# A transformer layer on one Trainium2 core: expert gate by tanh, normed rows stored modulated, low parts on VectorE, gathered rows handled ahead of the down-projection ring, the reciprocal root on GpSimd

## The chip, the core and the metric

The kernel runs on one core of a Trainium2 chip. The metric is device microseconds of one execution. A profile is one traced execution of the same program; its times are counted from the first instruction of the trace. TensorE has two clock levels, 2.4 and 1.2 GHz; the profile gives the granted level as a share, so 1.00 is 2.4 GHz and 0.50 is 1.2 GHz.

## The reference

One layer of a diffusion transformer over 2048 rows of width 1024 (and 256 context rows), in fp32: a mixer (latent attention with 8 heads, and bidirectional retention with 8 heads), then a mixture of experts in which each of 16 experts picks its own 256 rows, then a final norm.

```python
x = x + ga1 * y                                            # y: mixer output times w_o
h = rmsnorm(x, g_norm_ffn) * (1.0 + sc2) + sh2             # the modulated rows
aff = softmax(h @ w_router)                                # router, 16 experts
g, idx = top_k(swapaxes(aff, 1, 2), cap)                   # 256 rows for each expert
xs = h[idx]
a, u = xs @ w_gate, xs @ w_up                              # 1024 -> 768
y = (silu(a) * u) @ w_down * g                             # 768 -> 1024
x = x + ga2 * scatter_add(idx, y)
out = rmsnorm(x, g_final)
```

## The kernel before

The program is a chain of stages with a barrier between them: `modulation` (the row of `w_ada` products), `project`, `retention`, `attention`, `mix_out`, `experts` (a threshold search, then 16 expert turns) and `final_norm`. Every engine has its own instruction list, written by hand, and engines meet through semaphores; there is no scheduler. Within a list the order is fixed, so one late operation holds back all that stands behind it on its engine.

**Split products.** To keep fp32 accuracy on TensorE, each operand of a large product is split in two: a rounded part (ScalarE copies it to the round format) and a low part (the whole minus the rounded part, a subtraction on VectorE or GpSimd). Each product is three passes. The `whole` copy lies where the low part is written.

**Stage `mix_out`**, 16 tiles of 128 rows. On TensorE a turn m is: the first half of the product of the mixer output and `w_o` (L1280, 24 matmuls), the transposes of the normed rows of tile m-1 (L1289), the second half, the router of tile m-1 (L1297). VectorE adds the residual (L1384, L1386), scales by the reciprocal root (L1392), and after the transposes multiplies and adds the modulation by columns (L1359, L1361). ScalarE takes the sum of squares (L1331) and then the root as Ln and Exp (L1334, L1336). GpSimd makes the low part of the mixer tile (L1269). The unmodulated normed rows go to DRAM as `scratch_xn2`.

**Stage `experts`**, a turn for each expert e. TensorE: six steps `gate_up` of 96 matmuls each (L1614), the slot numbers of expert e+1 after the second (L1590), four blocks of transposes of the rows gathered for e+1 (L1600, two after `gate_up`, one after step 2 of `down` and one after step 3), and twelve steps `down` of six matmuls (L1628). The transposes go to two PSUM banks, 6 and 7, so block n waits until block n-2 has been read. VectorE reads each block with two operations `modulate` (L1818, L1820), ScalarE rounds it (L1665) and VectorE takes the low part (L1826). The gate of step f is exp on ScalarE (L1674) and four operations on VectorE (L1841, L1843 a reciprocal, L1845, L1848), then rounding (L1669) and the low part `rest_hidden` (L1852). Weights: `w_gate` and `w_up` come in three pieces of 2 MB in all each (L1498), the 12 pieces of `w_down` in a ring of six buffers of 256 KB (L1503): piece 6 is asked for when `down` step 0 is finished. Low parts: those of `w_gate` and of the first six pieces of `w_down` on VectorE (`rest_gate` L1830, `rest_down` L1835), those of `w_up` and of the last six pieces on GpSimd (`rest_up` L1540, `rest_down` L1545). GpSimd also issues the gather of e+1 (L1535) and the scatter-add of e (L1559), whose descriptors it writes itself. ScalarE alternates the rounding of `w_down` pieces 6 to 8 with that of gathered blocks 1 to 3.

**Stage `final_norm`**: four groups of four tiles: load, squares on ScalarE (L1966), Ln and Exp (L1969, L1971), scaling on VectorE (L1981), store.

## Time and profile before

| | before |
|---|---|
| median of 3 runs | 3539.53 us (3539.48 to 3540.74) |
| span of the profiled execution | 3526.4 us |
| TensorE matmul busy, share of the span | 3097.0 us, 88% |
| VectorE busy | 2266.7 us, 64% |
| ScalarE busy | 1427.3 us, 40% |
| GpSimd busy | 992.7 us, 28% |
| mean granted TensorE clock | 0.934 |
| HBM traffic over the span | 102 GB/s |

The page of the profile does not give the time of the profiled execution apart from its span. The span is 13.1 us shorter than the median of the runs; it counts from the first to the last instruction. The shares are means over stages with different limits, so the rows shown further down are read for each stage. A row of the window view gives the stretch and its length, then for TensorE, its weight loads, VectorE, ScalarE and GpSimd the busy us (with the number of instructions), the granted clock, the share of DMA time and GB/s. The expert turns begin at 2472.22 us and their last matmul ends at 3461.59 us.

### The profile page before, as it was taken

Reading aid. Unit: us, or ns where it says so; the run is one execution under the profiler, and the core shown is the slowest. Engines: PE = TensorE matmul, PEld = TensorE weight load, DVE = VectorE, ACT = ScalarE, POOL = GpSimd, SP = SyncE. Lnnn points to the kernel's source line nnn. Section 1 sums busy time; section 2 is a strip of 40 time slices with the busy share of each in tenths; the row PEclk is TensorE's granted clock in tenths of the full one; section 3 lists DMA queues with packets and bytes.
Section 4 is the critical chain, followed back from the end, with each engine's and each line's share of the span. In section 5 each row is a group of like instructions: output and inputs, shape, how many; then the busy total and the mean of one; then the engine's idle time right before and its main releaser. Section 6 shows DMA issues by size and latency. Waiting matters only on the chain. (4 is left out here: it accounts for less than half of the span.)

```text
span 3526.4 us, 44830 instructions
## 1 busy us (share of the span) xinstructions
PE 3097.0 (88%) x14689; PEld 2192.4 (62%) x14689; DVE 2266.7 (64%) x2823; ACT 1427.3 (40%) x2136; POOL 992.7 (28%) x514
## 2 busy tenths in 40 slices
PE   6899999999786999999999988971988989899892
PEld 1455555555785556556555647850888878888782
DVE  1133333333675777777777764557888989889893
ACT  0133333332223566666556644330334343333433
POOL 0000001100453332332333212211445444444441
PEclk9999999999776999999999999985999999999996
DMA  8412111121322011011001004341565666656656
GB/s 320 149 59 69 59 59 64 66 67 48 102 89 58 4 31 31 5 31 31 23 13 29 5 20 157 125 141 57 156 203 169 191 186 181 196 165 195 190 145 226
DMA packets 252530, 362.92 MB, mean 103 GB/s; under 512 B 34356, under 2 KB 168503, under 8 KB 250808
## 3 DMA queue, kind: packets, MB, share of 16 engines
q1 hardware_dynamic: 243128, 326.91, 28.5%
q0 software_dynamic: 9216, 33.56, 4.3%
q8 instruction: 113, 1.85, 0.2%
q14 instruction: 73, 0.60, 0.1%
HBM read 278.60 MB, written 81.83 MB: 102 GB/s over the span
## 5 line engine op out<-in xcount | busy, mean ns | idle before, releaser
L465 PE MATMUL bank<-w_in_sb,h_T 128*128 128x512 f32 (+1 forms) x1440 | 610.2, 579 | 2.1 <-DVE h_T L614 2.1
L1614 PE MATMUL ebank<-gathered_T,w_gate_up 128*128 128x256 f32 x4608 | 564.9, 284 | 20.5 <-ACT w_gate_up L1656 12.7
L1614 PEld LDWEIGHTS ebank<-gathered_T,w_gate_up 128*128 128x128 f32 x4608 | 560.2, 190 | 24.4 <-issue 23.5
L1075 PE MATMUL abank<-scores,head_v 128*128 128x512 f32 x1152 | 546.0, 602 | 2.2 <-ACT scores L1113 2.2
L1038 PE MATMUL abank<-head_qT,head_kT 96*128 96x512 f32 x1728 | 504.6, 437 | 22.9 <-POOL head_qT L1017 22.9
L465 PEld LDWEIGHTS bank<-w_in_sb,h_T 128*128 128x128 f32 x1440 | 271.1, 191 | 298.9 <-issue 298.7
L1038 PEld LDWEIGHTS abank<-head_qT,head_kT 96*128 96x128 f32 x1728 | 327.7, 190 | 169.9 <-issue 94.7
L1024 POOL TENSOR_TENSOR scores<-scores,max_for_pool 128x1536 f32<-128x1536 f32 x64 | 221.1, 3476 | 570.9 <-ACT max_for_pool L1107 570.9
L1101 ACT ACTIVATE scores<-abank 128x512 f32<-128x512 f32 x576 | 314.2, 608 | 77.0 <-PE abank L1038 71.2
L1075 PEld LDWEIGHTS abank<-scores,head_v 128*128 128x128 f32 x1152 | 218.6, 194 | 180.3 <-issue 162.8
L1628 PE MATMUL ebank<-w_down,hidden_T 128*128 128x512 f32 x1152 | 303.0, 418 | 21.0 <-POOL w_down L1545 20.8
L1540 POOL TENSOR_TENSOR w_gate_up<-w_gate_up_whole,w_gate_up 128x2048 fp32r<-128x2048 f32 x48 | 229.1, 4773 | 268.2 <-ACT w_gate_up L1656 180.0
L1113 ACT ACTIVATE scores<-scores 128x1536 f32<-128x1536 f32 x192 | 287.3, 1498 | 39.8 <-DVE scores L1155 35.5
L1139 DVE TENSOR_TENSOR score_max<-score_max,scores 128x1536 f32<-128x1536 f32 x128 | 225.1, 1758 | 94.4 <-ACT scores L1101 92.9
L1628 PEld LDWEIGHTS ebank<-w_down,hidden_T 128*128 128x128 f32 x1152 | 223.1, 199 | 80.0 <-POOL w_down L1545 30.2
L1155 DVE TENSOR_TENSOR scores<-scores,abank 128x1536 f32<-128x1536 f32 x128 | 218.1, 1744 | 52.0 <-PE abank L1058 52.0
L582 POOL TENSOR_TENSOR q_rope_terms<-q_rows,rope_rows 128x256 f32<-128x256 f32 x18 | 13.0, 724 | 788.1 <-ACT q_rows L552 788.1
L1674 ACT ACTIVATE gate_exp<-ebank 128x256 f32<-128x256 f32 x96 | 36.9, 384 | 453.2 <-DVE hidden_T L1852 237.9
L1280 PE MATMUL obank<-w_o_sb,mix_tile 128*128 128x512 f32 x768 | 184.7, 397 | 20.5 <-DVE w_o_sb L1399 20.5
L1545 POOL TENSOR_TENSOR w_down<-w_down_whole,w_down 128x512 fp32r<-128x512 f32 x96 | 124.0, 1304 | 275.8 <-ACT w_down L1660 275.2
L1656 ACT ACTIVATE w_gate_up<-w_gate_up_whole 128x2048 fp32r<-128x2048 f32 x96 | 176.3, 1900 | 16.6 <-DMA w_gate_up_whole<-in_w_exp_up 16.6
L1280 PEld LDWEIGHTS obank<-w_o_sb,mix_tile 128*128 128x128 f32 x768 | 143.8, 190 | 50.2 <-issue 21.3
(261 smaller groups left out, 4138.3 us busy)
## 6 DMA issues: line engine op xcount, KB each, us to landing
w_gate_up_whole<-in_w_exp_gate SPq DMA_DIRECT2D x48, 1024.0 KB, 5.9
w_gate_up_whole<-in_w_exp_up SPq DMA_DIRECT2D x48, 1024.0 KB, 9.0
w_down_whole<-in_w_exp_down SPq DMA_DIRECT2D x192, 256.0 KB, 2.9
ada_w<-in_w_ada SPq DMA_DIRECT2D x12, 2048.0 KB, 12.8
scratch_ret<-ret_rows SPq DMA_DIRECT2D x72, 256.0 KB, 2.5
x_tile<-in_x_all SPq DMA_DIRECT2D x18, 512.0 KB
w_in_sb<-in_w_in SPq DMA_DIRECT2D x4, 2048.0 KB, 15.0
chunk_qk<-scratch_ret SPq DMA_DIRECT2D x16, 512.0 KB
```

Of the source, the lines that this page charges most:

```text
L465: m = pe.matmul(banks[bank][:, 0:n], hT[u][:, k, :], w_in[:, k, lo:lo + n], start=(k == 0), stop=(k == KD - 1))
L1024: pool.tensor_tensor(x, x, mid(ms[:, :], G), ALU.subtract).then_inc(sg["shifted_pool"].sem, 1)
L1038: m = pe.matmul(banks[kt % 3][:, :], kT[u][:, kp, k], qT[u][:, qp, q], start=(n == 0), stop=(n == 2))
L1075: m = pe.matmul(banks[5 + j % 2][:, :], v1[u][:, kt, :], sc[j % 2][:, kt, :], start=(kt == 0), stop=(kt == T - 1))
L1101: act.activation(sc[j % 2][:, kt, :], banks[kt % 3][:, :], ACT.Copy).then_inc(sg["scores"].sem, 1)
L1113: act.activation(x, x, ACT.Exp, scale=ATT_SCALE).then_inc(sg["probs"].sem, 1)
L1139: dve.tensor_tensor(mx[:, :, :], mx[:, :, :], s[:, g * G:(g + 1) * G, :], ALU.max).then_inc(sg["max_keys"].sem, 1)
L1155: dve.tensor_tensor(x, x, mid(banks[4][:, :], G), ALU.subtract).then_inc(sg["shifted"].sem, 1)
L1280: x = pe.matmul(banks[2 * u + half][:, :], mt[u][:, mp, k, :], w_o[:, wp, k, half * 512:(half + 1) * 512], start=(k == 0 and n == 0), stop ...
L1540: pool.tensor_tensor(w_gu[c][:, 1, 1], w_gu_whole[c][:, 1, 1], w_gu[c][:, 0, 1].bitcast(F32), ALU.subtract).then_inc(sg["up_rest"].sem, 1)
L1614: x = pe.matmul(banks[f % 3][:, j * CAP:(j + 1) * CAP], w_gu[c][:, wp, j, k, o:o + P], xsT[:, xp, k, :], start=(k == 0 and n == 0), stop=( ...
L1628: x = pe.matmul(banks[Y_BANKS[2 * c + h]][:, :], hid[:, hp, k, h * P:(h + 1) * P], w_d[i % RING][:, wp, :], start=(k == 0 and n == 0), sto ...
```

## The change

Seven edits.

1. **Rows stored modulated.** `modulation` stores the 16 modulation columns (2048 numbers) to DRAM as two rows; the DMA has 128x16 runs of one number. `mix_out` loads them broadcast to all partitions (`ffn_rows`, 1 MB). The normed rows are multiplied and shifted before they are stored and transposed: the one operation L1392 becomes two (L1411, L1414 of the new kernel). The two pairs after the transposes become two copies (L1377), and `modulate` in `experts` goes: ScalarE and VectorE read the gathered block from PSUM.
2. **Mix root on GpSimd.** Ln and Exp on ScalarE become an add and a power of -0.5 on GpSimd (L1283, L1285).
3. **Transposes half a tile later.** TensorE's turn of `mix_out` becomes: first half, router of m-2, second half, transposes of m-1.
4. **Gate by tanh.** silu(a) = 0.5 a (1 + tanh(a/2)): one ScalarE operation and two on VectorE in place of four.
5. **Low parts on VectorE.** All of them: `rest_up` and GpSimd's `rest_down` go to VectorE. GpSimd keeps only gather and scatter in `experts`.
6. **Gathered rows ahead of the down ring.** ScalarE rounds gathered blocks 1 to 3 before pieces 6 to 11 of `w_down`; TensorE transposes the third and fourth block after `down` steps 1 and 2. A transpose block waits for the low part of the block two before.
7. **Final root on GpSimd**, as in 2.

```diff
@@ modulation, SP queue
+            sp.wait_ge(s_fold, 5)
+            sp.dma_start(scratch["ffn_rows"].rearrange("o (j p) -> p (o j)", p=P), perm["modcols"][:, 0, 24:40], allow_slow_non_contiguous=True).then_inc(perm["ffn_rows_stored"], 16)
             sp.wait_ge(s_ga2, 16)
@@ mix_out, GpSimd
+            def turn(m, u, behind, ahead):
+                sg["x2_rstd"].wait(pool, m, 1)
+                sg["x2_normed"].wait(pool, m - 1)
+                settled(pool)
+                pool.tensor_scalar(st[:, 1:2], st[:, 0:1], EPS, None, ALU.add).then_inc(sg["x2_rstd"].sem, 1)
+                sg["x2_rstd"].wait(pool, m, 2)
+                pool.tensor_tensor(st[:, 1:2], st[:, 1:2], power[:, 0:1], ALU.pow).then_inc(sg["x2_rstd"].sem, 1)
+                if ahead:
+                    mix_rest(m + 2, u)
@@ mix_out, TensorE
-                y_half(m, u, 0, first)
-                if not first:
-                    transposes(m - 1)
-                y_half(m, u, 1, first)
-                if not first:
-                    router(m - 1)
+                y_half(m, u, 0, behind == 0)
+                if behind == 2:
+                    router(m - 2)
+                y_half(m, u, 1, behind == 0)
+                if behind:
+                    transposes(m - 1)
@@ mix_out, VectorE
-                dve.tensor_scalar(xn[:, :], x2[u][:, :], st[:, 1:2], None, ALU.mult).then_inc(sg["x2_normed"].sem, 1)
+                dve.scalar_tensor_tensor(xs[:, :], x2[u][:, :], st[:, 1:2], ffn_rows[:, 1, :], ALU.mult, ALU.mult).then_inc(sg["x2_scaled"].sem, 1)
+                sg["x2_scaled"].wait(dve, m)
+                settled(dve)
+                dve.tensor_tensor(xn[:, :], xs[:, :], ffn_rows[:, 0, :], ALU.add).then_inc(sg["x2_normed"].sem, 1)
@@ experts, TensorE
-                sg["modulated"].wait(pe, e, 2 * (n - 2) + 1)
+                sg["gathered_rest"].wait(pe, e, n - 1)
...
-                    if i in (2, 3) and ahead:
-                        transposes(e + 1, i)
+                    if i in (1, 2) and ahead:
+                        transposes(e + 1, i + 1)
@@ experts, ScalarE
-                for i, n in ((6, 1), (7, 2), (8, 3)):
-                    round_down(e, i)
-                    if ahead:
+                if ahead:
+                    for n in range(1, 4):
                         round_gathered(e + 1, n)
-                for i in range(9, ND):
+                for i in range(6, ND):
                     round_down(e, i)
@@ experts, VectorE
-                dve.tensor_scalar(x[:, :], x[:, :], 1.0, None, ALU.add).then_inc(s.sem, 1)
-                s.wait(dve, e, 4 * f + 1)
-                dve.reciprocal(x[:, :], x[:, :]).then_inc(s.sem, 1)
-                s.wait(dve, e, 4 * f + 2)
-                dve.tensor_tensor(x[:, :], banks[f % 3][:, 0:CAP], x[:, :], ALU.mult).then_inc(s.sem, 1)
-                s.wait(dve, e, 4 * f + 3)
+                dve.scalar_tensor_tensor(x[:, :], x[:, :], 1.0, banks[f % 3][:, 0:CAP], ALU.add, ALU.mult).then_inc(s.sem, 1)
+                s.wait(dve, e, 2 * f + 1)
                 sg["d_psum"].wait(dve, e - 1)
-                dve.tensor_tensor(x[:, :], banks[f % 3][:, CAP:], x[:, :], ALU.mult).then_inc(s.sem, 1)
+                dve.scalar_tensor_tensor(x[:, :], x[:, :], 0.5, banks[f % 3][:, CAP:], ALU.mult, ALU.mult).then_inc(s.sem, 1)
```

**VectorE in an expert turn.** The rows of the second half of a turn before, from the low part of hidden step 4 to the fourth gathered block. `hidden_T` rows are `rest_hidden`, `gathered_T` rows the low parts of gathered blocks.

```order
L1852 TENSOR_TENSOR hidden_T<-gate_exp0,hidden_T 128x256
L1818 TENSOR_TENSOR modulated0<-ebank6,mod_cols 128x512
L1820 TENSOR_TENSOR modulated0<-modulated0,mod_cols 128x512
L1852 TENSOR_TENSOR hidden_T<-gate_exp1,hidden_T 128x256
L1818 TENSOR_TENSOR modulated1<-ebank7,mod_cols 128x512
L1820 TENSOR_TENSOR modulated1<-modulated1,mod_cols 128x512
L1826 TENSOR_TENSOR gathered_T<-modulated0,gathered_T 128x4x128
```

The same place of the changed kernel.

```order
L1843 TENSOR_TENSOR hidden_T<-gate_exp0,hidden_T 128x256
L1820 TENSOR_TENSOR gathered_T<-ebank6,gathered_T 128x4x128
L1843 TENSOR_TENSOR hidden_T<-gate_exp1,hidden_T 128x256
L1820 TENSOR_TENSOR gathered_T<-ebank7,gathered_T 128x4x128
L1830 TENSOR_TENSOR w_down0<-w_down0_whole_9521,w_down0 128x512
L1830 TENSOR_TENSOR w_down1<-w_down1_whole_9522,w_down1 128x512
```

The eight `modulate` operations are gone, the four low parts read PSUM, and six `w_down` low parts that were on GpSimd now stand between the gathered blocks and the output rows.

**TensorE in `mix_out`.** The rows of the last two turns and of what follows them, before. `w_o_sb` rows are half tiles, `x_normed` rows the transposes, `w_router_sb` rows the router.

```order
L1280 MATMUL obank<-w_o_sb,mix_tile 128x512 x24
L1289 MATMUL obank<-ident,x_normed 128x128 x8
L1280 MATMUL obank<-w_o_sb,mix_tile 128x512 x24
L1297 MATMUL obank<-w_router_sb,h_T 128x16 x8
L1289 MATMUL obank<-ident,x_normed 128x128 x8
L1297 MATMUL obank<-w_router_sb,h_T 128x16 x8
```

The same of the changed kernel, from the first half of the last tile on.

```order
L1302 MATMUL obank<-w_o_sb,mix_tile 128x512 x24
L1319 MATMUL obank<-w_router_sb,h_T 128x16 x8
L1302 MATMUL obank<-w_o_sb,mix_tile 128x512 x24
L1311 MATMUL obank<-ident,x_normed 128x128 x8
L1319 MATMUL obank<-w_router_sb,h_T 128x16 x8
L1311 MATMUL obank<-ident,x_normed 128x128 x8
```

Transposes have moved from between the two halves to behind them, and the router from behind the second half to between them, a tile later.

## Rows read from the trace of the kernel before

**Rows 1.** Windows of four expert turns; columns explained above.

```profile
2472.22:2533.49 61.27, 57.19 (x409) 52.51 (x410) 50.86 (x71) 23.76 (x35) 21.93 (x11) 0.96 0.50 164
...
2785.15:2849.66 64.51, 57.26 (x410) 52.35 (x408) 57.36 (x80) 26.37 (x36) 31.28 (x14) 0.95 0.62 188
2849.66:2909.04 59.38, 55.20 (x409) 50.49 (x409) 52.05 (x75) 21.32 (x33) 27.98 (x14) 1.00 0.63 188
...
3410.01:3461.59 51.58, 51.58 (x361) 47.95 (x359) 36.20 (x42) 13.62 (x26) 20.95 (x10) 1.00 0.24 62
```

**Rows 2.** Waits over the 16 turns: us in total, times, longest.

```profile
PE ebank L1600 <- DVE modulated L1818: 51.3, 21, 4.3
PE ebank L1628 <- POOL w_down L1545: 20.8, 21, 1.4
```

**Rows 3.** Timeline of TensorE in three turns: start us, us, operation, idle before.

```profile
2829.93 1.11 PE L1600 MATMUL ebank<-ident,gathered 128*128 128x128 f32 x4 [3.98 <-DVE modulated L1818]
2830.70 2.91 PE L1628 MATMUL ebank<-w_down,hidden_T 128*128 128x512 f32 x6
...
2885.30 1.04 PE L1600 MATMUL ebank<-ident,gathered 128*128 128x128 f32 x8
2886.09 4.46 PE L1628 MATMUL ebank<-w_down,hidden_T 128*128 128x512 f32 x18
...
3444.57 17.02 PE L1628 MATMUL ebank<-w_down,hidden_T 128*128 128x512 f32 x72
```

**Rows 4.** Timeline of GpSimd and VectorE where they work at once.

```profile
2502.99 6.02 POOL L1540 TENSOR_TENSOR w_gate_up<-w_gate_up_whole,w_gate_up 128x2048 fp32r<-128x2048 f32 x1 [9.26 <-ACT w_gate_up L1656]
2504.79 4.37 DVE L1841 TENSOR_SCALAR gate_exp<-gate_exp 128x256 f32<-128x256 f32 x1 [0.23 <-ACT gate_exp L1674]
...
2535.01 4.27 DVE L1830 TENSOR_TENSOR w_gate_up<-w_gate_up_whole,w_gate_up 128x2048 fp32r<-128x2048 f32 x1
2537.28 3.49 POOL L1559 DMA_INDIRECT scratch_acc<-expert_out,slot_tokens  x1
2539.40 3.42 DVE L1797 TENSOR_SCALAR one_hot<-slot_numbers_bf,slots_of_expert 128x256 bf16<-128x256 bf16 x16
2541.07 1.56 POOL L1559 DMA_INDIRECT scratch_acc<-expert_out,slot_tokens  x1 [0.30 <-issue]
```

**Rows 5.** Durations of two VectorE lines, ns minimum/median/maximum.

```profile
L1830 DVE TENSOR_TENSOR w_gate_up<-w_gate_up_whole,w_gate_up x48: 2276/2283/6704, 2452.9 to 3419.4; 128x2048 fp32r<-128x2048 f32 x48
L1852 DVE TENSOR_TENSOR hidden_T<-gate_exp,hidden_T x96: 414/417/4718, 2489.5 to 3448.7; 128x256 fp32r<-128x256 f32 x96
```

**Rows 6.** Timeline of ScalarE: the first refilled piece of the down ring.

```profile
2894.68 0.63 ACT L1660 ACTIVATE w_down<-w_down_whole 128x512 fp32r<-128x512 f32 x1 [0.83 <-DMA w_down_whole<-in_w_exp_down]
```

**Rows 7.** TensorE before the first expert turn.

```profile
2462.18 3.17 PE L1600 MATMUL ebank<-ident,gathered 128*128 128x128 f32 x12 [9.85 <-DMA gathered<-scratch_xn,slot_tokens]
```

**Rows 8.** `mix_out`: a wait in total, its end on TensorE, and GpSimd's power elsewhere.

```profile
PE obank L1289 <- DVE x_normed L1392: 9.5, 13, 5.4
...
2346.77 1.86 PE L1297 MATMUL obank<-w_router_sb,h_T 128*128 128x16 f32 x16
2354.07 1.97 PE L1289 MATMUL obank<-ident,x_normed 128*128 128x128 f32 x8 [5.44 <-DVE x_normed L1392]
...
L781 POOL TENSOR_TENSOR y_var<-y_var,minus_half x16: 1635/1635/1673, 912.0 to 1084.0; 128x8 f32<-128x8 f32 x16
```

**Rows 9.** Windows of the final stage, columns as in rows 1.

```profile
3483.00:3487.00 4.00, 0.00 (x0) 0.00 (x0) 0.00 (x0) 0.00 (x0) 0.00 (x0) 0.50 1.01 417
...
3519.00:3523.00 4.00, 0.00 (x0) 0.00 (x0) 3.97 (x4) 0.00 (x0) 0.00 (x0) 0.50 0.70 284
```

**Rows 10.** First ScalarE work of `project`, and its wait.

```profile
124.69 1.06 ACT L525 ACTIVATE square_out<-x_tile 128x1024 f32<-128x1024 f32 x1 [101.81 <-DMA x_tile<-in_x_all]
```

**Rows 11.** DMA queue from 2887 to 2895 us, then 8 to 13.5: packets, MB, share.

```profile
q1 hardware_dynamic: 2405, 2.73, 102.1%
...
q1 hardware_dynamic: 1021, 0.18, 16.2%
```

More of the change, by code:

```diff
@@ L1262, in _, with mix_rest @@
         def _(pool):
-            def turn(m, u, first, ahead):
+            def mix_rest(m, u):
                 x = mt[u]
@@ L1348, in _ @@
             loop(act, turn)
+            softmax(TM - 2)
             softmax(TM - 1)
@@ L1908, in _ @@
             for c in range(2):
-                rest_gate(0, c)
-            gathered(0)
+                rest_gate_up(0, c)
+            for n in range(4):
+                rest_gathered(0, n)
             loop(dve, turn)
```

170 lines of the change are left out of this document (77 added, 93 removed).

## The prediction

> **What bounds the kernel now.** I read the window view by expert turn first, then the waits of the 16 turns, then the timelines of the engines in one turn, and only then the two neighbours, `mix_out` and the final norm.
>
> Windows [rows 1]: TensorE is busy 55 to 57 us of every turn. The last turn, which prepares no successor, has no wait: 51.58 us, all busy. A quick turn takes 59.38 us, a slow one 64.51; fifteen turns take 3410.01 - 2472.22 = 937.8 us, 62.5 each. So TensorE sets the pace, and its waits are what can be won. VectorE is busy 50.9 to 57.5 us of these turns, which makes it the second limit.
>
> Waits [rows 2]: 51.3 us for `modulate` before the third and fourth block of transposes, 20.8 for GpSimd's low parts of `w_down`.
>
> A long wait costs twice. Behind one of 3.98 us, the next six `down` matmuls take 2.91 us [rows 3]; 72 of them in the last turn take 17.02, which is 1.42 for six. So they ran at the lower of the two clock levels, and the slow turn has a mean granted clock of 0.95, the quick one 1.00 [rows 1]. How TensorE falls behind is seen in the timeline of VectorE and GpSimd [rows 4]: a gate operation takes 4.37 us beside a GpSimd subtraction of 6.02, a `rest_gate` 4.27. Alone `rest_gate` takes 2.28, its longest 6.70; `rest_hidden` takes 0.417 in the median and 4.72 at most [rows 5]. VectorE and GpSimd hold each other up, hidden steps 4 and 5 come late, `modulate` stands behind them, and TensorE behind that.
>
> **The sum, expert turns.** First the turn without waits: `gate_up` and slots 2885.30 - 2849.66 = 35.6; two blocks of transposes 2886.09 - 2885.30 = 0.8; `down` 17.0; two more blocks 0.8 [rows 1, 3]. That is 54.2 us.
>
> Now what VectorE must do in it, by the durations of rows 5: 0.417 us for 256 columns and 2.283 for 2048 is 0.15 us plus 1.04 ns a column, so 0.68 for 512 and 1.2 for 1024. Six `rest_gate_up` 13.7; twelve `rest_down` 8.2; twelve gate operations 5.0; six `rest_hidden` 2.5; four gathered low parts 2.7; four output rows 2.8; one-hot 3.4 [rows 4]; slots and copies 1. Sum 39 of 54. The gate loses its reciprocal and one operation, `modulate` goes, and the low parts of GpSimd add 6.8 + 4.1. GpSimd has no subtraction left to hold VectorE up. ScalarE's order has no new table load in the loop, so I cost tanh as exp.
>
> Then each place at which TensorE could wait, in time from the start of the turn. (a) Slots at 11.6 need the one-hot: output rows of e-1 until 1.6, two `rest_gate_up` until 6.2, one-hot until 9.7. On time by 2. (b) Transposes of blocks 2 and 3, at 39.2 and 41.0 by the new order. `gate_up` ends at 35.6, tanh 36.1, two gate operations 37.1, `rest_hidden` 4 37.5; ScalarE rounds block 0 from 36.5 to 37.2, so its low part is done at 38.2, `rest_hidden` 5 at 38.6, block 1 at 39.3. Both waits go. (c) `down` step 6 is the new first one late. It is wanted 0.8 + 6 x 1.42 + 0.8 = 10.1 us after the end of `gate_up`. Its piece is asked for when step 0 ends, behind 2 MB of `w_gate` and `w_up`; in the quick turn ScalarE stood waiting for it until 2894.68, 9.4 after the end of `gate_up` [rows 3, 6]. Rounding 0.7, low part 0.7: 10.8. In that turn ScalarE had waited for the DMA, so a quicker order of rounding does not help. I take 0.6 us a turn, between 0 and 2 (if pieces 7 and 8 come late as well). Everything here needs the gather to have landed; it is issued at about 18, its blocks are wanted at 35.6.
>
> A turn then takes 54.8. The first has a slow start in either kernel (clock 0.96 and 61.27 us where a turn of its kind takes 59.4, rows 1): 56.8. Together 56.8 + 14 x 54.8 = 824.0, against 937.8: **gain 113.8 us**. The last turn stays.
>
> **The start of the turns.** From 2462.18 [rows 7] two blocks of transposes at 1.06 each (3.17 for three); block 0 is rounded (0.63) and its low part taken by 2464.9, block 2 follows, block 1 by 2466.0, block 3 until 2467.0, its rounding and low part until 2468.5. `gate_up` begins there, not at 2472.2: **gain 3.7**. VectorE's four `rest_gate_up` run until 2462, in the shadow of the gather. If they delay the gather's descriptors by one operation, 2.3 of it go.
>
> **`mix_out`.** TensorE waited 9.5 us for normed rows, 5.4 of them behind the last tile [rows 8]. The other 4.1 are won, as the transposes get half a tile more. At the end the last half tile finishes 4.1 + 0.85 earlier (the transposes of tile 14 have moved behind it). From there to the transposes of tile 15 it is 2354.07 - 2346.77 = 7.3 us now. Then: output and residual 0.7 + 1.2, squares about 1.3, the root p, two operations of 1.25, and 0.6 for the hand-overs: 6.3 + p; after the transposes two operations of 0.7 fewer. For p there is GpSimd's power over 8 columns, 1.64 us [rows 8]; for one column it lies between 0.1 and that, and the add is smaller. I take p = 1.2. Gain 4.1 + 0.85 + (7.3 - 7.5) + 1.4 = **6 us**, between 4 and 8. A GpSimd operation of 1.64 a tile has 14 us of room.
>
> **Final norm.** DMA runs at 417 GB/s until near its end [rows 9]: 17 MB in and out are its bound. Only the thin stretch at the end (284 GB/s in the window from 3519) is won by a shorter root: **2.5 us**, between 0 and 5.
>
> **The store of the modulation rows.** 2048 runs of one number, 128 for each DMA engine if spread evenly, stand ahead of the first x tile, and ScalarE's first work waits for exactly that tile [rows 10]. A run's time by rows 11: 16.2% of 16 x 5.5 us over 1021 packets is 14 ns where most are small; 102.1% of 16 x 8 us over 2405 is 54 ns where most have 1 KB. So 1.8 to 6.9 us. **Cost 3 us.**
> By the Trainium skill (DMA: Bandwidth & Descriptors, Specifications) a transfer under 512 B makes the DMA engine read, modify and write. That speaks for the upper end or above it; no row here shows a write of 4 bytes.
>
> Sum 113.8 + 3.7 + 6 + 2.5 - 3 = 123 us. The profiled span of 3526.4 becomes 3403.4. The runs' median is 13.1 above the span, and I keep that: **3416.5 us**.
>
> **Rivals.**
> 1. *The down ring becomes the bound.* With the turns closer together, pieces 7 and 8 land late as well. For: the DMA is full (102%) just then [rows 11]. Against: ScalarE found the second piece ready in all quick turns but had other work before it, so this is open. Two us a turn instead of 0.6: 3416.5 + 14 x 1.4 = 3436.
> 2. *VectorE is still held up by GpSimd.* Gather and scatter write their descriptors while VectorE now has far more subtractions. For: a scatter took 3.49 us beside `rest_gate` and 1.56 elsewhere [rows 4]. Against: the one-hot beside the second scatter took 3.42 for sixteen, and the first had to wait rather than VectorE. If each scatter held VectorE for 1.56, the one-hot would end at 12.8, and the slots wait 1.3 a turn: 3435.
> By the Trainium skill (SBUF — State Buffer, "SBUF: two separate sides") VectorE with two SBUF inputs and GpSimd share a port pair as an exclusive lock, and whoever starts second is blocked. The 4.37 and 4.27 us of rows 4 agree; it supports the gain and names this rival.
> 3. *The change does not take the stalls away.* VectorE's long durations would have another cause than GpSimd's subtractions, and hidden steps 4 and 5 stay as late as now. Then only the small terms remain, about 3530. Against it speaks that the longest durations stand beside GpSimd's in every row looked at.
> 4. *The store of single numbers is slow: slower than before.* If each engine finishes a run before it starts the next, 128 times a DMA's round trip stand before the first x tile. It decides against the change from 129 / 128 = 1.0 us a run on, twenty times the 54 ns of rows 11; at 1.4 us it gives 3416.5 + 176 = 3593. If the runs are pipelined but all on one engine, 2048 x 14 to 54 ns is 29 to 111 us, and the change is still ahead.
>
> **Chances.** Forecast with its bounds (3402 to 3430) 0.68. Rivals 1 and 2, alone or together (3430 to 3455), 0.20. A store that costs tens of us (3440 to 3525) 0.06. Rival 3 0.03, of which a third within 0.2%. Rival 4 0.02; some other loss 0.01. The likeliest 3416; the range from 3400, where neither the ring nor the store costs anything and the power is cheap, to 3442, into rivals 1 and 2. About 0.2% (7 us) is what a measurement of this kernel can tell from no change: faster 0.96, same 0.01, slower 0.03.
>
> **What would show it.** Turns of 54.5 to 55.5 us, all alike, with a granted clock of 1.00; no wait of the transposes for VectorE; a wait of about 0.6 us before `down` step 6 for a VectorE low part; `rest_gate_up` at 2.28 and `rest_hidden` at 0.42 on the mean too; VectorE busy near 39 us a turn. In `mix_out` GpSimd's power under 1.6 us and one short wait at the end. ScalarE's first work in `project` 3 us later. I am wrong if turns still differ by 5 us, if several `down` steps wait, or if the first x tile comes more than 10 us later.

## The result

The changed kernel takes 3459.17 us, the median of four runs (3445.06 to 3461.21), against 3539.51 before: a ratio of 0.9765, with a 95% interval of 0.9744 to 0.9785. The forecast was 3416.5 with a range of 3400 to 3442: the direction is right, the time is 43 us over. The profiled execution has a span of 3459.3 us.

Stage by stage, in the two profiles (us; a stage ends where the next one's first TensorE or ScalarE row stands):

| stretch | before | after | difference | forecast |
|---|---|---|---|---|
| up to the first work of `project` | 124.69 | 133.62 | +8.9 | +3 |
| `project` | 767.2 | 767.4 | +0.3 | 0 |
| `retention` (no line changed) | 218.6 | 226.2 | +7.6 | 0 |
| `attention`, load of `w_o` | 1013.5 | 1014.4 | +0.9 | 0 |
| `mix_out`, first product to end of last router | 237.7 | 267.2 | **+29.5** | -6 |
| search, to the first transposes of `experts` | 100.6 | 93.9 | -6.7 | 0 |
| start of the turns | 10.0 | 6.3 | -3.8 | -3.7 |
| 15 expert turns | 937.8 | 836.1 | **-101.7** | -113.8 |
| last turn | 51.6 | 51.6 | 0 | 0 |
| end of the last turn to the end | 64.8 | 62.5 | -2.3 | -2.5 |
| span | 3526.4 | 3459.3 | -67.1 | -123 |

The page of the changed kernel, busy time by engine:

```profile
PE 3088.8 (89%) x14689; PEld 2190.0 (63%) x14689; DVE 1967.8 (57%) x2631; ACT 1371.3 (40%) x2056; POOL 646.6 (19%) x412
```

**Expert turns.** Windows of a quick turn and a slower one, columns as in [rows 1]:

```profile
2735.88:2790.74 54.86, 54.40 (x408) 50.64 (x409) 36.82 (x66) 22.37 (x34) 6.83 (x4) 1.00 0.70 210
2790.74:2847.18 56.44, 54.74 (x410) 50.30 (x408) 37.60 (x68) 24.92 (x35) 6.89 (x4) 1.00 0.69 209
```

The waits over all 16 turns (us in total, times, longest), where [rows 2] had 51.3 for `modulate` and 20.8 for GpSimd's low parts:

```profile
ACT w_down L1665 <- DMA w_down_whole<-in_w_exp_down: 61.0, 32, 4.0
PE ebank L1633 <- DVE w_down L1830: 14.3, 17, 1.9
PE ebank L1619 <- DVE gathered_T L1820: 1.7, 1, 1.7
PE ebank L1619 <- issue: 0.9, 3, 0.5
```

And VectorE's two lines of [rows 5], with minimum, median and maximum in ns:

```profile
L1825 DVE TENSOR_TENSOR w_gate_up<-w_gate_up_whole,w_gate_up x93: 2278/2284/2293, 2499.9 to 3354.5; 128x2048 fp32r<-128x2048 f32 x93
L1843 DVE TENSOR_TENSOR hidden_T<-gate_exp,hidden_T x96: 411/418/426, 2524.5 to 3381.7; 128x256 fp32r<-128x256 f32 x96
```

The maximum is now the median: the 6.70 and 4.72 us of [rows 5] are gone. TensorE's granted clock is 1.00 in the slower turn too. What is left is a wait for the down ring: the second row says that TensorE waits for VectorE's low part, the first that behind it stands a DMA. Of the 14.3 us, 13.5 stand before `down` step 6 and 0.8 before step 7.

**`mix_out`.** TensorE in one tile of the changed kernel, from the transposes on (start, duration, operation, idle before):

```profile
2276.18 1.04 PE L1311 MATMUL obank<-ident,x_normed 128*128 128x128 f32 x8
2276.97 5.73 PE L1302 MATMUL obank<-w_o_sb,mix_tile 128*128 128x512 f32 x24
2284.00 2.03 PE L1319 MATMUL obank<-w_router_sb,h_T 128*128 128x16 f32 x16 [1.30 <-issue]
2285.86 7.23 PE L1302 MATMUL obank<-w_o_sb,mix_tile 128*128 128x512 f32 x24
```

And VectorE beside it:

```profile
2276.38 0.69 DVE L1398 TENSOR_TENSOR x_tile<-obank,ga_rows 128x512 f32<-128x512 f32 x1 [5.41 <-PE obank L1302]
2277.11 1.22 DVE L1402 TENSOR_TENSOR x_tile<-x_tile,x_again 128x1024 f32<-128x1024 f32 x1
2278.25 1.28 DVE L1377 COPY h_T<-obank 128x512 f32<-128x512 f32 x2
2280.78 1.29 DVE L1411 SCALAR_TENSOR_TENSOR x_scaled<-x_tile,x_stats,ffn_rows 128x1024 f32<-128x1024 f32 x1 [1.26 <-POOL x_stats L1285]
2282.22 1.23 DVE L1414 TENSOR_TENSOR x_normed<-x_scaled,ffn_rows 128x1024 f32<-128x1024 f32 x1 [0.15 <-DVE x_scaled L1411]
2283.37 0.16 DVE L1387 RECIPROCAL router_stats<-router_stats 128x1 f32<-128x1 f32 x1
2283.66 0.24 DVE L1389 TENSOR_SCALAR affinities<-router_exp,router_stats 128x16 f32 x1
```

The router product starts 0.1 us after VectorE has written the affinities of the tile before (2283.90). They stand last in VectorE's turn, behind both operations on the normed rows, and these behind squares and root. From the output of the second half to there it is 7.5 us; TensorE has 0.8 us of transposes and 5.7 of products to fill it. The profile calls the wait "issue" nine times and names the affinities five times; one of the nine, 6.64 us, is the router of tile 14 behind the last half tile. In the kernel before, the affinities stood last in VectorE's turn as well, and came even later, 7.8 us after the output of the second half:

```profile
2277.17 0.69 DVE L1384 TENSOR_TENSOR x_tile<-obank,ga_rows 128x512 f32<-128x512 f32 x1 [1.08 <-PE obank L1280]
2284.75 0.24 DVE L1373 TENSOR_SCALAR affinities<-router_exp,router_stats 128x16 f32 x1
2291.01 1.86 PE L1297 MATMUL obank<-w_router_sb,h_T 128*128 128x16 f32 x16
```

But there the router that needs them came 6.0 us after they were written. TensorE asked for them 14.0 us after the end of that half tile; in the new order it asks after 6.5. The wait costs twice: the half tile behind it takes 7.23 us where the one before took 5.73. The window view has the granted clock of the two:

```profile
2276.97:2282.50 5.53, 5.53 (x27) 4.41 (x25) 4.09 (x6) 1.40 (x4) 0.79 (x2) 1.00 0.55 186
2285.86:2292.93 7.07, 7.07 (x25) 5.66 (x26) 0.17 (x1) 0.00 (x0) 1.69 (x2) 0.77 0.00 0
```

TensorE was at the higher level (2.4 GHz) all through the first, and for part of the second at the lower (1.2). The Trainium skill describes a kernel whose array idles for moments between groups of matmuls and goes back and forth between the two levels (TensorE: Matmul & The Clock Gate, "A second HAM failure mode: psum-queue depth-cycling"); the trace agrees with it: 1.00 in the half tile ahead of the wait and 0.77 in the one behind it.

**The store.** SyncE's issues, then ScalarE's first work in `project`, which in [rows 10] stands at 124.69 behind a wait of 101.81:

```profile
120.02 0.38 SPq L230 DMA_DIRECT2D scratch_ffn_rows<-mod_cols  x1
121.34 0.36 SPq L413 DMA_DIRECT2D x_tile<-in_x_all  x1
133.62 1.06 ACT L527 ACTIVATE square_out<-x_tile 128x1024 f32<-128x1024 f32 x1 [111.06 <-DMA x_tile<-in_x_all]
```

**The search.** Nothing in it was changed, and it became 6.7 us shorter. In the kernel before, GpSimd's first two low parts fall into it:

```profile
2380.26 4.54 POOL L1540 TENSOR_TENSOR w_gate_up<-w_gate_up_whole,w_gate_up 128x2048 fp32r<-128x2048 f32 x1 [48.51 <-ACT w_gate_up L1656]
2380.81 4.06 DVE L1723 TENSOR_TENSOR search_candidates<-threshold,search_steps 128x48 uint32<-128x48 uint32 x1 [0.39 <-DVE search_steps L1736]
2386.28 4.50 POOL L1540 TENSOR_TENSOR w_gate_up<-w_gate_up_whole,w_gate_up 128x2048 fp32r<-128x2048 f32 x1 [1.47 <-ACT w_gate_up L1656]
2387.66 3.80 DVE L1735 COPY_PREDICATED threshold<-search_keep,search_candidates 128x16 uint32<-128x16 uint32 x3
2391.94 0.21 DVE L1723 TENSOR_TENSOR search_candidates<-threshold,search_steps 128x48 uint32<-128x48 uint32 x1 [0.39 <-DVE search_steps L1736]
```

VectorE's candidates take 0.21 us elsewhere and 4.06 here, its three copies 0.83 elsewhere (2379.50) and 3.80: 3.85 + 2.97 = 6.8 us, the whole difference. Runs 6 and 7 below test it.

### The profile page after: what moved, and what is told of

The parts are those of the page before. It is cut to its first block and busy times, and to the rows that moved or that the text cites. A ratio compares the mean times of both kernels' runs of the same rounds, so it can differ in the third digit from the quotient of the medians.

```text
span 3459.3 us, 44130 instructions
## 1 busy us (share of the span) xinstructions
PE 3088.8 (89%) x14689; PEld 2190.0 (63%) x14689; DVE 1967.8 (57%) x2631; ACT 1371.3 (40%) x2056; POOL 646.6 (19%) x412
## 5 line engine op out<-in xcount | busy, mean ns | idle before, releaser
L1633 PE MATMUL ebank<-w_down,hidden_T 128*128 128x512 f32 x1152 | 286.4, 402 | 14.3 <-DVE w_down L1830 14.3
L1633 PEld LDWEIGHTS ebank<-w_down,hidden_T 128*128 128x128 f32 x1152 | 213.2, 189 | 68.8 <-DVE w_down L1830 20.8
L1825 DVE TENSOR_TENSOR w_gate_up<-w_gate_up_whole,w_gate_up 128x2048 fp32r<-128x2048 f32 x96 | 215.3, 2285 | 13.4 <-ACT w_gate_up L1661 13.4
L1302 PE MATMUL obank<-w_o_sb,mix_tile 128*128 128x512 f32 x768 | 200.2, 421 | 21.2 <-DVE w_o_sb L1421 21.2
L1567 POOL DMA_INDIRECT scratch_acc<-expert_out,slot_tokens x32 | 73.6, 2298 | 628.9 <-DVE expert_out L1849 624.0
L1302 PEld LDWEIGHTS obank<-w_o_sb,mix_tile 128*128 128x128 f32 x768 | 154.9, 205 | 55.7 <-issue 22.0
L584 POOL TENSOR_TENSOR q_rope_terms<-q_rows,rope_rows 128x256 f32<-128x256 f32 x18 | 13.1, 726 | 797.6 <-ACT q_rows L554 797.6
```

The source lines that it names most:

```text
L1302: x = pe.matmul(banks[2 * u + half][:, :], mt[u][:, mp, k, :], w_o[:, wp, k, half * 512:(half + 1) * 512], start=(k == 0 and n == 0), stop ...
L1633: x = pe.matmul(banks[Y_BANKS[2 * c + h]][:, :], hid[:, hp, k, h * P:(h + 1) * P], w_d[i % RING][:, wp, :], start=(k == 0 and n == 0), sto ...
L1825: dve.tensor_tensor(w_gu[c][:, 1, j], w_gu_whole[c][:, 1, j], w_gu[c][:, 0, j].bitcast(F32), ALU.subtract).then_inc(sg["gu_rest"].sem, 1)
```

## The experiments

Medians, and ratios against the kernel before, timed in the same rounds; the stages in us from the profile of each run. "Run 1" and the like are the numbers of this table; "edit 1" and the like belong to the list of the change. In the diffs the signals at the ends of lines are left out.

| kernel | median | ratio, 95% interval | `mix_out` | search | 15 turns |
|---|---|---|---|---|---|
| before | 3539.5 | 1 | 237.7 | 100.6 | 937.8 |
| changed | 3459.2 | 0.9765 [0.9744, 0.9785] | 267.2 | 93.9 | 836.1 |
| 1 probabilities early | 3414.1 | 0.9639 [0.9616, 0.9661] | 228.4 | 93.9 | 831.1 |
| 2 store late | 3450.2 | 0.9737 [0.9713, 0.9761] | 267.5 | 93.8 | 832.7 |
| 3 third chunk behind the ring | 3466.9 | 0.9789 [0.9763, 0.9815] | 267.5 | 93.8 | 844.9 |
| 4 TensorE's order of before | 3422.3 | 0.9664 [0.9641, 0.9687] | 232.8 | 94.1 | 831.4 |
| 5 order of 4, root on ScalarE | 3477.7 | 0.9831 [0.981, 0.9852] | 287.6 | 93.9 | 835.3 |
| 6 low parts on GpSimd | 3488.8 | 0.9864 [0.9841, 0.9886] | 267.1 | 100.4 | 860.2 |
| 7 before, low parts on VectorE | 3533.5 | 0.9994 [0.9982, 1.0007] | 237.7 | 93.7 | 947.0 |
| 8 exp gate | 3509.4 | 0.9921 [0.989, 0.9951] | 267.5 | 93.9 | 888.2 |
| 9 before, tanh | 3471.6 | 0.9812 [0.9788, 0.9836] | 237.5 | 100.9 | 882.8 |
| 10 runs 1 and 2 together, third chunk behind three | 3468.3 | 0.9817 [0.9797, 0.9837] | 228.4 | 94.1 | 893.4 |
| 11 runs 1 and 2 together | 3404.8 | 0.9626 [0.9605, 0.9647] | 228.1 | 94.0 | 832.6 |
| 12 as 11, third chunk split | 3401.9 | 0.962 [0.9598, 0.9642] | 228.7 | 93.8 | 827.9 |

**1. Probabilities early.** The two small operations that write the affinities move ahead in VectorE's turn; ScalarE takes the exp of that softmax ahead of the squares, which the excerpt leaves out.

```diff
     dve.tensor_tensor(x2[u][:, c], banks[2 * u + half][:, :], perm["ga1"][:, c], ALU.mult)
     if half == 0 and behind == 2:
         largest(m - 2)
+        probabilities(m - 2)
...
-    if behind == 2:
-        probabilities(m - 2)
```

> The changed kernel with one edit in mix_out: VectorE writes the probabilities of tile m-2 right after that tile's largest, between the two gate products, and not behind the normed rows; ScalarE takes that softmax ahead of the squares. Theory A (TensorE's router of tile m-2 waits for the probabilities of tile m-3, which stand behind the whole normed-row chain, 1.2 to 1.3 us a tile, and the stall lowers the granted clock for the half tile after it, 7.3 us for 5.7): both go, a tile comes back from some 16.6 us to 13.7 to 14, the 6.64 us before the router of tile 14 shrink to under 2, and the stage from 267 us to 230 to 240; the kernel some 27 to 35 us below the changed one. Rival B (the longer chain over GpSimd itself holds the stage): the wait only moves to the transposes or to VectorE, and the stage stays above 255 us. Rival C (the attention tiles, which ScalarE waits 73.6 us for, come too late): the stage stays above 255 us and TensorE waits for mix_tile.

Measured: `mix_out` 228.4 us, the kernel 45 us below the changed one. Its TensorE in the same place:

```profile
2275.45 5.74 PE L1302 MATMUL obank<-w_o_sb,mix_tile 128*128 128x512 f32 x24
2281.02 1.86 PE L1319 MATMUL obank<-w_router_sb,h_T 128*128 128x16 f32 x16
2282.73 5.71 PE L1302 MATMUL obank<-w_o_sb,mix_tile 128*128 128x512 f32 x24
```

No idle time, and no longer half tile. A tile takes 13.6 us. Theory A holds, and B and C fall: the chain over GpSimd is as long as it was (7.0 us from the output to the normed rows in either kernel), and ScalarE still waits for the attention tiles, but TensorE waits for neither. Of the 45 us 38.8 are this stage; the turns, the same code, were 5.0 shorter as well. In the six profiles with that code (the changed kernel, 1, 2, 4, 5, 11) they take 831.1 to 836.1 us, so that much is chance.

**2. Store late.** The store goes from the end of `modulation` to the attention stage, behind `load(1, 1)`.

> The changed kernel with the store of the modulation rows issued in the attention stage, behind its first loads, and no longer ahead of the first x tile. If the 2048 pieces of 4 bytes hold the queue in front of the x tile and of the last w_in parts (the changed kernel's first row of the projection starts at 133.6 us, before's at 124.7), the projection starts at 124 to 126 us again, 8 to 9 us are won, and the attention stage keeps its length of 966.6 us from first to last score-value product. If the store's cost is elsewhere (its extra wait on SyncE), it starts at 130 us or later.

```profile
125.47 1.06 ACT L525 ACTIVATE square_out<-x_tile 128x1024 f32<-128x1024 f32 x1 [102.80 <-DMA x_tile<-in_x_all]
```

8.15 us of the 8.9 come back, and the attention stage keeps its 967 us. The other 0.8 were lost ahead of it in this run: from the issue of the x tile to this work it is 3.4 us here (issued at 122.10) and 3.5 before (121.21), but 12.3 in the changed kernel (121.34). The store's extra wait on SyncE went with it in this run, but it is not the cost: the x tile was issued only 0.13 us later than before. The queue in front of the x tile is the cost.

**3 and 10. The third gate and up chunk behind the down ring.** SyncE loads it behind all six `w_down` loads (3), or behind the first three of them (10, with edits 1 and 2).

```diff
-    if ahead:
-        for c in range(NG):
-            sg["gu_psum"].wait(sp, e, 2 * c + 2)
-            load_gate_up(e + 1, c)
     for i in range(RING, ND + RING if ahead else ND):
+        for c in range(NG):
+            if ahead and GU_AT[c] == i:      # (6, 6, 12) in 3, (6, 6, 9) in 10
+                sg["gu_psum"].wait(sp, e, 2 * c + 2)
+                load_gate_up(e + 1, c)
         sg["d_psum"].wait(sp, e, i - RING + 1)
```

> The changed kernel with the loads of the next expert's third gate and up chunk issued behind the six w_down loads of the down stage, not ahead of them. Theory D (in every other expert turn the seventh w_down tile lands late because 2 MB of gate and up weights stand ahead of it in the queue, 1.6 to 1.9 us a turn): the ScalarE wait for w_down of 61.0 us in 32 times falls under 25 us, the turns are even at 54.8 to 55.0 us, and the 15 turns take 823 to 826 us in place of 836.1; some 10 us below the changed kernel. Rival (the third chunk is then late itself): TensorE waits for w_gate_up at the fourth product or ScalarE holds the first tanh back, and the turn is 56 us or more.

> Three edits on the changed kernel together: probabilities of tile m-2 right after its largest, the store of the modulation rows in the attention stage, and the third gate and up chunk loaded behind three of the six w_down loads (behind all six it came too late). If the gains are in separate stages they add up: mix_out 228 us (267 in the changed kernel), the projection's start 9 us earlier, and, if the third chunk now neither delays the seventh w_down tile nor comes late itself, expert turns of 54.0 to 54.8 us, 15 of them 812 to 824 us in place of 836: in all 3459 - 39 - 9 - 12 to 24, some 3385 to 3402 us. If the load order only trades one wait for the other, the 15 turns stay at 830 to 845 us and the kernel comes out at 3405 to 3415 us.

Both missed. Run 3 fits its rival in size (56.3 us a turn). Run 10 is worse than its rival too: the waits were traded, but for larger ones, and the 15 turns take 893.4 us, not 830 to 845. In 3 TensorE's `w_down` wait is gone (ScalarE's is not: 59.3 us, 61 times, 2.2 at most), but the chunk comes late: ScalarE waits for it 14 times, 37.0 us in all. TensorE waits 20.0 us in six times:

```profile
2846.52 3.72 ACT L1663 ACTIVATE w_gate_up<-w_gate_up_whole 128x2048 fp32r<-128x2048 f32 x2 [3.12 <-DMA w_gate_up_whole<-in_w_exp_up]
2847.72 13.22 PE L1621 MATMUL ebank<-gathered_T,w_gate_up 128*128 128x256 f32 x96 [3.36 <-issue]
```

TensorE's wait is not for this chunk, though. The first products of a turn read the first chunk, and the six waits (3.1 to 3.6 us) all stand at the start of turns 2, 4, 6, 8, 10 and 12 (counted from 0), where the program's loop over two turns begins again. At the starts of the odd turns from 1 to 13 ScalarE waits 1.8 to 2.6 us for the chunk too, TensorE waits for nothing, and the first tanh comes 6.0 to 6.1 us into the turn, as in the changed kernel. The DMA view of the 3.36 us from 2844.36 on shows a second queue:

```profile
q1 hardware_dynamic: 727, 1.25, 103.1%
q8 instruction: 1, 0.02, 2.1%
```

The one packet of the queue `instruction` (16 KB) begins 0.3 us after TensorE has fallen idle, and TensorE goes on 3.0 us behind its start. At all six waits it is 2.96 to 3.02 us from packet to product. In the changed kernel such a packet comes while TensorE is still at work. So it looks as if TensorE waited for its own instructions, which were read late while the weights filled the DMA; no run tests this.

In 10 it is the tenth `w_down` tile, now behind the 2 MB with less time left, and the wait brings the lower clock, so that 18 matmuls take 7.11 us, where by the 17.02 of [rows 3] for 72 they take 4.3:

```profile
2868.03 2.00 ACT L1665 ACTIVATE w_down<-w_down_whole 128x512 fp32r<-128x512 f32 x3 [7.02 <-DMA w_down_whole<-in_w_exp_down]
2869.44 7.11 PE L1633 MATMUL ebank<-w_down,hidden_T 128*128 128x512 f32 x18 [3.10 <-DVE w_down L1830]
```

**4. TensorE's order of before in `mix_out`**, rows still modulated on VectorE, root still on GpSimd:

```diff
     y_half(m, u, 0, behind == 0)
-    if behind == 2:
-        router(m - 2)
-    y_half(m, u, 1, behind == 0)
-    if behind:
-        transposes(m - 1)
+    if behind:
+        transposes(m - 1)
+    y_half(m, u, 1, behind == 0)
+    if behind:
+        router(m - 1)
```

> The changed kernel with TensorE's order of before in mix_out: transposes of tile m-1 between the halves of tile m, its router behind the second half, the copies, the largest and the softmax one tile earlier again; the rows stay modulated on VectorE and the root stays on GpSimd. Theory A (the new place of the router is what costs): the transposes wait for the normed rows, whose chain is some 1.3 us longer than before, 6.8 us against a half tile of 5.7; 1 to 2 us of wait a tile, a tile of 15 to 17 us, the stage 245 to 265 us. Rival B (the chain is the whole of the loss, the order does nothing): the same 265 to 270 us as the changed kernel. If the order alone were at fault and the chain short enough, it would be before's 237.7 us or less.

The copies for the router, the largest and the softmax move a tile earlier with it. Better than expected: 232.8 us, 5 less than before. I had taken the chain to be 1.3 us longer than before. It is shorter: from the output of the second half to the end of the normed rows it is 7.0 us here and in the changed kernel, 7.3 to 7.4 before. The transposes wait 7.1 us in all, of it 5.4 behind the last tile, and the granted clock is 1.00 from 2160 to 2340 us. The new order with run 1's edit is only 4.4 us better than this; as it was written, it was 34.4 worse.

**5. The root on ScalarE, in the order of 4.** Ln and Exp come back behind the squares, GpSimd's two operations go.

> TensorE's order of before in mix_out (as in the earlier run of that edit, stage 232.8 us) with the root of x2 back on ScalarE by Ln and Exp, the rows modulated on VectorE. What the place of the root is worth where the transposes stand half a tile behind the rows: by the rows of before two table loads of 1.28 us and two short steps, 3.1 us, against some 1.2 to 2.4 us on GpSimd. The transposes then wait 1 to 2 us a tile, the stage is 245 to 262 us. If the root's place is nothing, it stays within 2 us of 232.8.

287.6 us, beyond the range I gave: 55 us for the place of one root. The waits of 5, with those of 4 beneath them:

```profile
DVE x_scaled L1410 <- ACT x_stats L1352: 70.1, 16, 4.4
PE obank L1305 <- DVE x_normed L1413: 38.5, 16, 7.4
```

```profile
DVE x_scaled L1411 <- POOL x_stats L1285: 37.3, 16, 2.4
PE obank L1311 <- DVE x_normed L1414: 7.1, 2, 5.4
```

The chain to the normed rows is 9.0 to 9.1 us instead of 7.0, and nearly all of that is a wait of 1.9 to 2.0 us in each tile, as expected. 31 us of the 55 are waits. The products of the stage take 202.6 us instead of 184.7, which is 18 more, at a mean granted clock of 0.91 instead of 1.00 in the middle of the stage; the rest, 5.1 us, lies in the transposes. I had priced the wait and not the clock behind it.

**6 to 9. Which part of the change shortens the expert turn.** 6 is the changed kernel with the low parts of the up weights and of the last six `w_down` tiles on GpSimd, as before. 7 is the kernel before with them on VectorE. 8 is the changed kernel with the four-step gate by exp. 9 is the kernel before with the two-step gate by tanh. The core of 7 and of 9:

```diff
+for j in range(2):
+    dve.tensor_tensor(w_gu[c][:, 1, j], w_gu_whole[c][:, 1, j], w_gu[c][:, 0, j].bitcast(F32), ALU.subtract)
...
+for i in range(6, ND):
+    rest_down(e, i)
```

```diff
-dve.tensor_scalar(x[:, :], x[:, :], 1.0, None, ALU.add)
-dve.reciprocal(x[:, :], x[:, :])
-dve.tensor_tensor(x[:, :], banks[f % 3][:, 0:CAP], x[:, :], ALU.mult)
-dve.tensor_tensor(x[:, :], banks[f % 3][:, CAP:], x[:, :], ALU.mult)
+dve.scalar_tensor_tensor(x[:, :], x[:, :], 1.0, banks[f % 3][:, 0:CAP], ALU.add, ALU.mult)
+dve.scalar_tensor_tensor(x[:, :], x[:, :], 0.5, banks[f % 3][:, CAP:], ALU.mult, ALU.mult)
```

> The changed kernel with the low parts of the up weights and of the last six w_down tiles computed by GpSimd again, as before; the tanh gate, the rows stored modulated and the new order stay. Theory L (the two engines hold each other off at the port: 4.5 us steps on VectorE, and GpSimd's low parts come late; this made the turn of 62.5 us): the 15 turns come back to 900 us or more, VectorE's 128x2048 subtraction again has steps of 4 to 6 us, and the search before the experts takes some 100.6 us instead of 93.9. Rival (VectorE's own work, the four steps of the gate and the modulation, was the load that held the turn): the turns stay under 860 us in 15.

> The kernel before with one part of the change: all low parts on VectorE, none on GpSimd; the exp gate in four steps, the modulation of the gathered rows, the order of the down ring and mix_out stay as before. Theory L (the port is nearly all of it): the search takes 93.9 us, and the 15 expert turns fall from 937.8 to 840 to 880 us. Rival (VectorE gets more work than it had waits, 8 modulation steps and 12 gate steps a turn more than in the changed kernel, some 12 us): the turns stay above 900 us, and the cheaper gate and the stored rows are what makes room.

> The changed kernel with the gate by exp and its four steps on VectorE (the reciprocal takes 1.75 us) in place of tanh and two steps. By the rows VectorE works 36.8 us in a turn of 55.7 in the changed kernel; the four steps add 13 us, 50 us. Theory V (VectorE's load in the stretch around the turn's end holds TensorE up; the low parts went to VectorE at no price only because the gate became cheap): the stalls at the transposes and at w_down come back, 15 turns of 860 to 920 us in all. Rival (the low parts on one engine are enough, the gate hides): 836 to 845 us.

> The kernel before with one part of the change: the gate by tanh in two steps. Low parts shared with GpSimd, modulation in the expert turn, mix_out all as before. Theory V: the gate's 13 us less on VectorE are most of what the turn gains, the 15 turns 865 to 895 us (937.8 before, 860.2 with the rows stored modulated too), and the search still takes 100.6 us. Rival: the modulation steps right ahead of the transposes are what holds TensorE, and the turns stay over 910 us.

Theory L falls as I put it, with the lock as nearly all of the stall. The search answers to it alone (93.7 and 93.9 us without GpSimd's subtractions, 100.4 to 100.9 with them), but the turns do not: 7 takes 9 us more than the kernel before, not 60 to 100 less, and 6 lands at the rival's edge (860.2). Theory V holds in 8 and in 9. Windows over the 15 turns of before, 7, 9, 8, 6 and the changed kernel, the third busy time VectorE's, the fifth GpSimd's:

```profile
2472.22:3410.01 937.79, 850.55 (x6120) 778.20 (x6121) 823.91 (x1149) 357.36 (x511) 431.19 (x193) 0.96 0.61 184
```

```profile
2474.27:3421.24 946.97, 853.63 (x6120) 780.63 (x6121) 805.05 (x1284) 361.26 (x512) 98.12 (x58) 0.96 0.60 183
```

```profile
2473.56:3356.36 882.80, 843.67 (x6120) 768.80 (x6121) 623.58 (x969) 355.08 (x512) 449.62 (x193) 0.98 0.64 195
```

```profile
2508.50:3396.67 888.17, 837.67 (x6120) 776.07 (x6121) 730.66 (x1164) 360.57 (x511) 98.10 (x58) 0.97 0.64 195
```

```profile
2516.08:3376.23 860.15, 825.64 (x6120) 766.21 (x6121) 492.52 (x849) 363.59 (x512) 424.52 (x193) 0.99 0.66 201
```

```profile
2509.02:3345.16 836.14, 820.15 (x6120) 761.08 (x6121) 547.96 (x984) 362.87 (x511) 98.04 (x58) 0.99 0.68 206
```

VectorE works 54.9 us a turn before and 53.7 in 7: the lock's delay goes and the low parts take its place. Run 7 does not show that the lock was cheap. If I take from each VectorE operation of the 15 turns the median of its line and shape, 153 us are left before (10.2 a turn), 6 in 7 and 4 in the changed kernel; and the low parts that 7 adds come to 10.9 us a turn. So 7 exchanges two loads of one size. No run took the low parts off GpSimd without giving them to VectorE. In 7 TensorE waits 40.7 us for `modulate` and 48.8 for VectorE's low parts of `w_down`. One operation fills VectorE there, the gate's reciprocal (minimum, median, maximum in ns):

```profile
L1826 DVE RECIPROCAL gate_exp<-gate_exp x71: 1752/1753/1755, 2554.0 to 3271.6; 128x256 f32<-128x256 f32 x71
```

That is 10.5 us in a turn of six. The other forms of this size take 0.42. The Trainium skill says of it that it divides by a step repeated eight times (VectorE: DVE Perf Modes, "First, the fixed hardware budget"); 1.75 against 0.42 agrees that it is a slow one, no run here shows its inside. With the tanh gate the turns lose 55.0 us on the kernel before (9) and 52.0 on the changed one (8 against it). The gate alone takes the stall at the transposes away and brings it back. Of TensorE's two large waits before (51.3 us for `modulate`, 20.8 for GpSimd's low parts) the first does not occur in 9 and the second does; in 8, with all low parts on VectorE, the wait at the transposes returns. The first row is of 9, the second of 8:

```profile
PE ebank L1628 <- POOL w_down L1545: 21.5, 16, 2.5
PE ebank L1606 <- DVE gathered_T L1820: 46.7, 15, 3.7
```

Low parts on VectorE are worth 24.0 with the tanh gate (6 against the changed kernel) and cost 9.2 without it. The rows stored modulated and the earlier gathered rows were not parted; 9 against 6 gives both together 22.7.

**11 and 12. The two fastest versions.** 11 is the changed kernel with the edits of runs 1 and 2. 12 also parts the third chunk: `w_gate` ahead of the `w_down` loads, `w_up` behind three of them.

> The two edits that paid, together, on the changed kernel, with its own load order: mix_out 228 us, the projection's start 8 to 9 us earlier, the 15 expert turns 830 to 836 us. 3459 - 39 - 9 = 3411 us with the run-to-run scatter of the retention stage (218.6 to 227.4 us in the runs so far, the code being the same); 3400 to 3412 us.

> As the first kernel of this call, with the third chunk's load parted: the gate half stays ahead of the w_down loads, the up half goes behind three of them. Theory Q (what stands in the queue ahead of a w_down load delays it; 2 MB cost 1.6 us at the seventh tile, and 3 to 4 us at the tenth because less time is left there): with 1 MB at either place the seventh tile comes in time and the tenth is late by under 1 us: 15 turns of 812 to 826 us. Rival (the order of issue does not matter, the bytes of the down stage do): a wait of 1 to 3 us at the tenth tile, 840 us or more.

11 takes 3404.8 us, within what was expected. 12 takes 3401.9; their intervals overlap, and only the turns of the profile speak for it (827.9 against 832.6 in 11, and 3.2 below the lowest of the six profiles with the old load order). It missed the 812 to 826 by 2 us. Of theory Q the part on the down ring holds: TensorE does not wait at the seventh tile, and at the tenth 0.1 to 0.6 us in five turns and 1.7 in one. What is left are six waits at the start of a turn, 0.8 to 2.1 us each:

```profile
PE ebank L1621 <- issue: 7.0, 6, 2.1
PE ebank L1635 <- DVE w_down L1832: 3.9, 6, 1.7
```

They stand where the six of run 3 stand, at the start of every second turn, and ScalarE waits for no gate and up chunk in these turns at all. So they are not the late `w_up`; no run tests what they are. The two last prepared turns, 54.2 and 54.0 us, are about as short as this turn gets. How to load the 9 MB of weights of a turn so that all have that length stays open.

## Why the prediction was wrong, step by step

**`mix_out`: the step that failed** is the sum "4.1 + 0.85 + (7.3 - 7.5) + 1.4 = 6 us". It prices the new order by the transposes alone and puts the router's wait at nothing, without a reason. "The other 4.1 are won, as the transposes get half a tile more" did come true: the transposes wait for nothing in the changed kernel. But I did not follow the router, which moved with them. It now stands between two halves, and asks for the affinities of the tile before it 6.5 us after the end of a second half, no longer 14.0. The affinities stand where they stood, at the end of VectorE's turn, behind a chain that I had worked out myself for the last tile. What the runs show in place of the gain is a wait of 1.2 to 1.3 us in each tile, 1.5 us of slower products behind it, and 6.6 us before the router of tile 14. -6 forecast, +29.5 measured: 35.5 of the 56 us by which the span missed. Run 1 shows it. Without that wait the stage gains 4.9 us in the old order (run 4) and 9.3 in the new (run 1), around the 6 that I had, with bounds of 4 to 8. p was 0.57 us and the add 0.22, within the bounds; I took 1.2.

**Expert turns.** Both stalls went, the turn without waits (54.2) is right (54.0 in runs 3 and 12), VectorE's 39 us were 36.5. 12.1 us too little gained. The term that was mis-sized is the wait for the down ring: 14.3 us in the 15 turns for the 9.0 of my sum. Before step 6 it is 0.4 to 0.6 us in eight turns, 1.6 to 1.9 in five and 0.3 and 0.7 in two, inside its bounds of 0 to 2; step 7 waits in two turns, 0.8 us together, so rival 1 came in small part. Five more waits at `gate_up`, 3.4 us together, were in no term. The other 3.4 us are products that took longer than the 2 us that I had for the slow start; in one turn the mean granted clock was 0.97. The profiles scatter by 5 us here, so this division is no finer than that. Rival 2 did not come: TensorE never waits for the slots, and VectorE's operations keep their medians.

The reason that I gave for the stalls was incomplete: "VectorE and GpSimd hold each other up" is true for 10.2 us a turn, but the stall at the transposes was VectorE's load as a whole, of which the reciprocal was another 10.5, and run 9 ends it with the lock still there. Of the two rows of [rows 4] that I took for the lock, the operation of 4.37 us has one input in SBUF, so my sentence on two inputs covers only the one of 4.27. The sum held because it counted every operation of VectorE, whichever the reason.

**Start of the turns and final norm**: 3.8 for 3.7, 2.3 for 2.5.

**The store**: 8.9 us for 3, above the upper bound of 6.9 and beneath rival 4's. The bound was 54 ns a number on each DMA engine, the time of a packet of mostly 1 KB; measured are about 70. The rule that I had from the Trainium skill (DMA: Bandwidth & Descriptors, Specifications) pointed to this side, and the 8.9 us agree; no run here shows the mechanism. In rival 4 the store decides against the change from 126 us on (123 and the 3 of the sum), not 129; that is still 1.0 us a run.

**The search**: 6.7 us that I did not count. The lock of [rows 4] was at work in a stage that the change does not touch, and I read its rows only where the turns were. In run 6, with GpSimd's subtractions back, the search takes 100.4 us again; in run 7, the kernel before without them, 93.7.

**The offset.** I kept 13.1 us between the profiled span of before and the median. In the changed kernel the run's own time is 3461.07 for a span of 3459.3, 1.8 apart. The rest of the 13.1 is that the execution profiled before was one of the shorter ones. `retention`, the same code in all, took 218.5 to 227.4 us in the fourteen profiles of this study. Before and changed kernel, with the granted clock after the busy times:

```profile
891.86:1110.44 218.58, 166.09 (x1088) 158.70 (x1089) 132.83 (x158) 54.00 (x98) 102.80 (x83) 0.72 0.32 94
```

```profile
901.06:1127.25 226.19, 169.64 (x1088) 161.85 (x1089) 132.82 (x158) 53.77 (x98) 103.53 (x83) 0.70 0.31 91
```

So the span missed by 55.9 us (`mix_out` 35.5, turns 12.1, store 5.9, `retention` and what follows it 8.8, less the search's 6.7, with 0.3 left), and the 13.1 took a part of it back by chance. Of the 7.6 us in `retention` 3.6 are TensorE's busy time at the lower mean clock; what the other 4 are stays open.

## What to carry to other kernels

When an operation of one engine is moved, list every wait of each operation that moves with it, and ask when on the other engines its signal is given, and how long before it is now asked for; a result of 0.4 us behind a chain of 7 cost this kernel 39. Price a wait on TensorE with the clock that it takes with it, in `mix_out` 1.3 us of idle time and 1.5 of slower products. Before crediting a lock or a port with a stall, add up the busy time of the engine behind it, and what the cure gives that engine to do: here it was full, and it took a cheaper operation to make room.

## What the hardware showed that I had not expected

- A store of 2048 separate numbers of 4 bytes held the next DMA of the same queue back by 8.8 to 8.9 us (12.3 us from its issue to the work on it, 3.4 to 3.5 without the store), 4.3 ns a number for the whole queue.
- VectorE's reciprocal over 128x256 takes 1.753 us, four times another operation of that shape (0.417).
- Two GpSimd subtractions of 4.5 us each cost VectorE's search 3.85 and 2.97 us, with VectorE's operations of 0.2 us stretched to 4.06 and 3.80 for three.
- Behind a wait of 1.30 us the granted clock was 0.77 over the next half tile of `mix_out`; in runs 1 and 4, without the wait, it was 1.00 from tile to tile.
- The trace has packets of 16 KB of a queue `instruction` among the loads. At the six places in run 3 where the loop begins again, with the other queue at 103% in the one shown, such a packet began 0.0 to 0.6 us after TensorE had fallen idle, and TensorE went on 3.0 us after the packet's start.
- `retention`, the same code, differs by 9 us between executions (218.5 to 227.4); its mean granted clock was 0.72 in one of 218.6 us and 0.70 in one of 226.2.
